# A decoder layer on one core: two projections of the input matrix by seven half-size products, with the operand sums made by ScalarE copies and adding transfers

## What is computed

```python
h = rms_norm(x, ln_mix_g[l])
a_q, a_k, a_v, b_a, b_g, c_q, c_kv, c_kr, d_u = jnp.split(h @ w_in[l], split_at, axis=-1)
q = rms_norm(a_q.reshape(b, s, SWA_HEADS, SWA_HEAD_DIM), swa_qn_g[l])
o_a = swa_sink_attention(q, k, v, swa_sinks[l], rel_bias)
o_b = conformer_conv(b_a, b_g, ...)
o_c = mla_attention(c_q, c_kv, c_kr, ...)        # c_q is RMS-normalised first
o_d = s5_mixer(d_u, ...)
x = x + o @ w_out[l]
x = x + memory_cross_attention(rms_norm(x, ln_cross_g[l]), rms_norm(mem, mem_ln_g[l]), ...)
x = x + hier_moe(rms_norm(x, ln_moe_g[l]), ...)  # top-1 group, top-2 of 32 experts
```

## Time and profile before

| | us |
|---|---|
| three timed runs, median (lowest to highest) | 1413.32 (1412.78 to 1415.44) |
| the profiled execution | 1413.58 |
| its span | 1411.8 |
| PE busy in the span | 1210.6 (86%) |
| DVE busy | 593.1 (42%) |
| ACT busy | 208.4 (15%) |
| GpSimd busy | 13.9 (1%) |
| bytes moved | 477.79 MB, mean 338 GB/s |

### The profile page before, as it was taken

How to read it: one execution, slowest core, us unless ns; L and a number is a source line. 1 busy time by engine, 2 the same in 40 slices (tenths; PEclk the granted TensorE clock), 3 DMA queues, 4 the chain that set the end, 5 groups by cost and what they waited for, 6 DMA issues and landing times.

```text
span 1411.8 us, 16085 instructions
## 1 busy us (share of the span) xinstructions
PE 1210.6 (86%) x6731; PEld 566.3 (40%) x6731; DVE 593.1 (42%) x1222; ACT 208.4 (15%) x461; POOL 13.9 (1%) x31
## 2 busy tenths in 40 slices
PE   8999999999999999887667978777878687787777
PEld 4785565656885632322222222222322222222223
DVE  5999984858754442331122322222222222222222
ACT  3311023351022411100000000000001000000001
POOL 3000000000000000000000000000000000000000
PEclk9999999999999999998888988888889878988898
DMA  9343454333556879999999999999999999999998
GB/s 288 140 150 132 155 190 169 130 120 138 180 239 233 308 312 431 432 431 434 429 431 431 430 431 428 433 431 431 430 431 432 431 431 430 430 431 430 431 424 318
DMA packets 62728, 477.79 MB, mean 338 GB/s; under 512 B 13701, under 2 KB 21253, under 8 KB 45504
## 3 DMA queue, kind: packets, MB, share of 16 engines
q1 hardware_dynamic: 61392, 476.40, 81.8%
q0 software_dynamic: 864, 0.25, 0.3%
q10 hardware_dynamic: 400, 0.10, 0.0%
HBM read 474.63 MB, written 2.11 MB: 338 GB/s over the span
## 4 chain that ended last, share of the span: by engine, by line
PE 58%; DMA 36%; DVE 3%; ACT 2%; issue 1%; SPq 1%; DVEq 0%; ACTq 0%
DMA ring<-in_moe_w_up_dram 20%; DMA late_ring<-in_moe_w_up_dram 14%; PE bank L1294 11%; PE bank L733 10%; PE bank L1329 7%; PE bank L748 5%; PE bank L1050 5%; PE bank L1315 2%; PE bank L717 2%; PE bank L1253 2%; PE bank L1174 2%; PE bank L798 2%; PE bank L1130 2%; PE bank L1019 2%; DMA ring<-in_moe_w_down_dram 1%; PE bank L1366 1%
## 5 line engine op out<-in xcount | busy, mean ns | idle before, releaser
L1294 PE MATMUL bank<-ring,x_gathered 128*32 128x512 f32 x1184 | 252.2, 680 | 52.0 <-DMA late_ring<-in_moe_w_up_dram 36.0
L1294 PE MATMUL bank<-late_ring,x_gathered 128*32 128x512 f32 x800 | 202.3, 682 | 38.8 <-DMA ring<-in_moe_w_up_dram 37.4
L2760 DVE TENSOR_TENSOR tokens_out<-tokens_out,bank 128x512 f32<-128x512 f32 x240 | 148.5, 680 | 202.6 <-PE bank L1366 202.6
L2743 DVE SCALAR_TENSOR_TENSOR hidden<-hidden,bank 128x128 f32<-128x128 f32 x31 | 8.9, 287 | 338.8 <-ACT hidden L1898 338.8
L733 PE MATMUL bank<-ring,hT 128*128 128x512 f32 (+2 forms) x384 | 142.1, 530 | 0.1
L1294 PEld LDWEIGHTS bank<-ring,x_gathered 128*32 128x32 f32 x1184 | 67.0, 123 | 142.2 <-issue 137.5
L1253 PE MATMUL bank<-x_tok,select 128*32 128x512 f32 x512 | 115.9, 1032 | 7.3 <-DVE select L2652 4.2
L1329 PE MATMUL bank<-ring,hidden 128*32 128x512 f32 x560 | 89.1, 793 | 18.2 <-DVE hidden L2745 18.2
L733 PEld LDWEIGHTS bank<-ring,hT 128*128 128x128 f32 x384 | 72.7, 190 | 66.9 <-issue 59.6
L1294 PEld LDWEIGHTS bank<-late_ring,x_gathered 128*32 128x32 f32 x800 | 53.3, 123 | 111.4 <-issue 108.9
L1366 PE MATMUL bank<-y_slots,weight_slots 32*128 32x512 f32 x496 | 72.0, 651 | 28.8 <-ACT y_slots L1913 21.0
(11 more groups left out here) (472 smaller groups left out, 1235.0 us busy)
## 6 DMA issues: line engine op xcount, KB each, us to landing
ring<-in_moe_w_up_dram SPq DMA_DIRECT2D x19, 4096.0 KB, 40.3
ring<-in_moe_w_down_dram SPq DMA_DIRECT2D x16, 4096.0 KB, 29.6
ring<-in_moe_w_gate_dram SPq DMA_DIRECT2D x16, 4096.0 KB, 38.9
late_ring<-in_moe_w_down_dram SPq DMA_DIRECT2D x13, 4096.0 KB, 29.6
late_ring<-in_moe_w_gate_dram SPq DMA_DIRECT2D x12, 4096.0 KB, 39.6
late_ring<-in_moe_w_up_dram SPq DMA_DIRECT2D x10, 4096.0 KB, 38.1
ring<-in_w_in_dram SPq DMA_DIRECT2D x20, 1024.0 KB, 8.1
ring<-in_w_out_dram SPq DMA_DIRECT2D x16, 1024.0 KB, 6.5
```

The lines of the kernel that those rows point to most:

```text
L1294: mm = pe.matmul(gu_bank[SLOTS * c:SLOTS * c + SLOTS, :], XGT[:, at, n % 4, n // 4, :], pieces[c % 2][:, FF * (n % 8):FF * (n % 8) + FF], ...
L2760: ins = v.tensor_tensor(y, x, mix[c][:, :], ALU.add)
```

## The change

The two projections `cq` and `sq` are each cut in four by halves: tokens (0, 1), contraction (two sides of eight slices, 0 and 1) and columns (two halves of 256). With seven products of 128 tokens x 1024 x 256 columns (`seven`, eight matmuls of 256 moving columns each) instead of eight, and sums and differences of the operands and of the results, the same 256 x 512 block comes out.

- **Token sums** T1 to T4 (128 x 8 x 128, 0.5 MB) are made once and used by both groups; **weight sums** S1 to S4 (128 x 8 x 256, 1 MB) once for each group. Each sum is made in two steps: ACT copies one operand, with its sign, to the place of the sum (`part`, L1757 of the new kernel, semaphore `parts_ready`), and GpSimd issues a transfer that adds the other operand to it (`accumulate`, `accum_op=add`); for the token sums from `hT` in SBUF, for the weight sums from `w_in` in HBM once more. 12 copies and 12 adding transfers, 10 MB in all. S2 is made from S1 and S4 from S2 (sign turned by the copy), and GpSimd issues S3 after S1 has landed and S2 after S3 has landed.
- PE takes the products of a group in the order a0, b0 (on plain operands), d1 (T3, S3), c (T1, S1), b1 (T4), a1 (T2, S2), d0 (S4).
- ACT drains four banks for each group; DVE joins them by five operations (`join_seven`).
- **Order.** The groups are now loaded and multiplied in the order ckv, skv, `y1`, cq, sq. `mT0` and `mT1` follow one another directly. SP loads sq pieces 2 and 3, which take the place of cq pieces 0 and 1, after product c of cq.
- The gains of the memory tokens get a tile of their own; the two early constants share one semaphore, so DVE waits for both before its first use of one of them.

Diff, cut:

```diff
-    w = [(g, q) for g in ("u", "za", "zg", "cq", "ckv", "sq", "skv") for q in range(4)]
+    w = [(g, q) for g in ("u", "za", "zg", "ckv", "skv", "cq", "sq") for q in range(4)]
...
+        T8 = [scr[:, a:a + 1024].rearrange("p (k t) -> p k t", k=8) for a in (10240, 8192, 11264, 9216)]
+        S8 = {"cq": [eights(GB[:, :]), eights(scr[:, 0:2048])], "sq": [eights(scr[:, 2048:4096]), eights(GB[:, :])]}
...
-                    if g in ("za", "sq") and q < 2:
+                    if g in ("za", "skv") and q < 2:
                         sp.wait_ge(s["half_used"], 1 if g == "za" else 2)
+                    elif g in ("cq", "sq") and q < 2:
+                        wait_filled(sp, g + "c")
...
-                sp.dma_start(KF[:, :], const_d[:, N_KEPT:N_CONST]).then_inc(s["front_const_in"], 16)
+                sp.dma_start(KF[:, :], const_d[:, N_KEPT:N_CONST]).then_inc(s["const_in"], 16)
...
+            def accumulate(ready, dst, src, name):
+                pool.wait_ge(s["parts_ready"], ready)
+                pool.dma_start(dst, src, accum_op=ALU.add).then_inc(s[SUMMED[name][0]], 16)
...
+            accumulate(1, t1, hT8(1, 1), "T1")
+            accumulate(2, c1, block8_source("cq", 0, 1), "cqS1")
+            accumulate(3, t3, hT8(0, 0), "T3")
+            wait_sum(pool, "cqS1")
+            accumulate(4, block8("cq", 0, 1), block8_source("cq", 1, 1), "cqS3")
+            accumulate(5, t2, hT8(0, 0), "T2")
+            wait_sum(pool, "cqS3")
+            accumulate(6, c2, block8_source("cq", 1, 1), "cqS2")
+            accumulate(7, t4, hT8(1, 0), "T4")
+            wait_sum(pool, "T3")
+            accumulate(8, q1, block8_source("sq", 0, 1), "sqS1")
+            accumulate(9, block8("cq", 1, 0), block8_source("cq", 1, 0), "cqS4")
+            wait_sum(pool, "T4")
+            accumulate(10, block8("sq", 0, 1), block8_source("sq", 1, 1), "sqS3")
+            accumulate(11, q2, block8_source("sq", 1, 1), "sqS2")
+            accumulate(12, block8("sq", 1, 0), block8_source("sq", 1, 0), "sqS4")
...
-            projection("cq", 512)
+            def seven(g):
+                def by8(b, x, w):
+                    for j in range(8):
+                        mm = pe.matmul(b, x[:, j, :], w[:, j, :], start=j == 0, stop=j == 7)
+                    return mm
...
+                by8(a[:, 0:T], hT8(0, 0), block8(g, 0, 0))
+                by8(b[:, 0:T], hT8(1, 0), block8(g, 1, 0)).then_inc(s["half_used"], 1)
+                wait_sum(pe, "T3")
+                wait_sum(pe, g + "S3")
+                by8(d[:, T:2 * T], t3, block8(g, 0, 1))
+                wait_sum(pe, "T1")
+                wait_sum(pe, g + "S1")
+                filled(by8(c[:, 0:T], t1, s1))
+                wait_sum(pe, "T4")
+                filled(by8(b[:, T:2 * T], t4, block8(g, 1, 1)))
+                wait_sum(pe, "T2")
+                wait_sum(pe, g + "S2")
+                filled(by8(a[:, T:2 * T], t2, s2))
+                wait_sum(pe, g + "S4")
+                filled(by8(d[:, 0:T], hT8(1, 1), block8(g, 1, 0)))
             projection("ckv", 320)
-            projection("sq", 512)
             projection("skv", 256)
+            c_products(1)
+            seven("cq")
+            seven("sq")
             pe.wait_ge(s["mem_in"], 16)
             model_transposes("mT", 0, xn_of[0])
-            c_products(1)
...
+            act.wait_ge(s["scan_done"], 5)
+            part(t1, hT8(0, 1), 1.0)
+            pieces_arrived("cq", 0)
+            part(c1, block8("cq", 0, 0), -1.0)
+            part(t3, hT8(0, 1), -1.0)
+            part(block8("cq", 0, 1), block8("cq", 0, 1), -1.0)
             act.wait_ge(s["dist_out"], 16)
             for tt in range(TT):
                 drain(f"skv{tt}", SKV[:, tt, :], cols=256, scale=ROWS[:, tt:tt + 1])
+            act.wait_ge(s["scan_done"], 8)
+            wait_sum(act, "T1")
+            part(t2, t1, -1.0)
+            drain("y1", OT[:, 14:16, :], four(2))
+            wait_sum(act, "cqS1")
+            part(c2, c1, -1.0)
+            wait_sum(act, "T2")
+            part(t4, t2, 1.0)
+            pieces_arrived("sq", 0)
+            part(q1, block8("sq", 0, 0), -1.0)
+            wait_sum(act, "cqS2")
+            act.wait_ge(s["half_used"], 3)
+            part(block8("cq", 1, 0), c2, -1.0)
+            part(block8("sq", 0, 1), block8("sq", 0, 1), -1.0)
+            wait_filled(act, "cqc")
+            wait_sum(act, "sqS1")
+            part(q2, q1, -1.0)
+            drain_seven("cq")
+            wait_sum(act, "sqS2")
+            act.wait_ge(s["half_used"], 4)
+            part(block8("sq", 1, 0), q2, -1.0)
+            drain_seven("sq")
...
-            wait_task(dve, "ckv1")
+            join_seven("cq")
...
-            wait_task(dve, "skv1")
+            join_seven("sq")
```

83 lines of the change are left out of this document (65 added, 18 removed).

## The result

| | before | after |
|---|---|---|
| timed runs, median (lowest to highest), us | 1413.38 (1412.78 to 1415.44) | 1450.48 (1447.48 to 1454.21) |
| ratio, 95% interval | | 1.0259 (1.0247 to 1.0272) |
| profiled execution, us | 1413.58 | 1447.92 |
| its span, us | 1411.8 | 1446.0 |

The change costs 37 us. It was forecast to cost 16, with 1447 as the upper end of the range: the direction was right, the size was not.

A forecast was written before the change was run, and what follows sets the result against it. PE was taken to bound the front, one to one to the end: -6.9 + 0.5 + 1.2 + 19.9 = +14.7, with about 1.5 for slower pieces and clock +16, from 1413.6 to 1430 us; range 1409 to 1447.

The forecast's parts named there:

- Removed and added on PE, -6.9: Projections cq and sq on PE: seven half-width products save 3.4 us a group, 6.9 us in all, if no product waits.
- Order and transposes, +0.5 and +1.2: PE waits about 0.5 us for skv's late pieces, and 1.2 us ahead of xv0 for the drains of mT0.
- One to one to the end: A microsecond on PE in the front moves the end by one, since early expert loads wait for a PE task.
- DVE's joins at nothing: Five join operations a group on DVE, 2.6 us, lie under other work and cost nothing; uncovered, 5 us.
- S1's start, 140: cq's first weight sum is issued at 140 us, after cq piece 1 arrives, T1's transfer and a copy of about 2.0 us.
- Landings: 1 MB adding transfers land in 8.3 us, plus 2.6 sharing for S1 and S4; waits in d1, b1, d0 total 19.9 us.
- "The group sq has its sums made in that time and I give it no wait.": sq's operand sums are made during cq's waits, so sq's products on PE wait 0 us.
- Clock after waits, 1.5 with the slower pieces: Lower TensorE clock after waits, together with the slower 1 KB pieces, adds about 1.5 us.
- Constants, nothing: The joint wait for two constants delays DVE's early work by half a microsecond under PE's work, at no cost.
- Signs of being wrong: Landings of 5 us, S transfers not slowed by SP's loads, or a later front without a later end.
- the two rules weighed ahead: Adding transfers run at about half a copy's rate (5.2 us of data), against GpSimd's 2.0 us plus bytes at 436 GB/s (4.4 us).
- three turns: Rival: two reads and the write in turn, 10.9 us an adding transfer, d0 35 us late, 1446 us; chance 0.17 (or worse).

The follow-up runs named there:

- narrow_first: Kernel before the change with only the new order (ckv, skv, y1, cq, sq as plain projections, memory transposes in a row): 1416.44 us.
- no_transfers: Changed kernel without its 12 adding transfers, TensorE waiting only for ScalarE's copies; stretch from zg1's end to xv0 87.84 us, whole time (1443.67 us) not comparable.
- gpsimd_adds: Changed kernel with the 12 sums made by GpSimd additions on blocks already in SBUF, without copies or transfers: 1455.3 us.
- loads_later: Changed kernel with SyncE issuing the first piece of sq only after cqS3 has landed: 1453.99 us.
- price_probe: Changed kernel with four more GpSimd transfers, run one by one in idle stretches (512 KB and 1 MB, each plain and adding): 1447.84 us.
- const_merged: Kernel before the change with only the edit to the constants (one shared semaphore, waits for both loads): 1414.37 us.
- s1_early: Changed kernel with cqS1 made early, from a block loaded at about 54 us, its adding transfer in the idle stretch behind 87 us: 1442.14 us.
- one_block_early: Changed kernel with only cq by seven products, behind sq's plain projection; cqS1 made before the projections, cqS2 issued before cq's pieces arrive: 1422.14 us.
- plain_copies_b: Changed kernel with GpSimd's 12 transfers as plain copies, same places and waits, run once more for a profile: 1432.8 us.

## Why the prediction was wrong, and where it was right

- **Removed and added on PE, -6.9.** Right: 6.87 us between narrow_first and no_transfers.
- **Order and transposes, +0.5 and +1.2.** Right: 0.63 and 1.30 us of waits; narrow_first's stretch has 0.7 us more, which stays unplaced.
- **One to one to the end.** Right: 1211.1 to 1212.1 us behind xv0 in every kernel that routes alike, gpsimd_adds apart.
- **DVE's joins at nothing.** Right: the five operations of cq's join took 2.7 us (205.06 to 207.74), and PE waits for no norm.
- **S1's start, 140.** It was 142.46: piece 1 landed at 140.16, not 137 to 138, and ScalarE's copy came behind that. T1's transfer is the smaller part of it: in no_transfers, which has none, the copy starts at 139.39 instead of 140.25. The four pieces themselves took about 12 us from their release, not 10.
- **Landings: the step that failed.** The data term of an adding transfer, at half a copy's rate, was right (8.3 assumed, 8.9 alone; in the changed kernel cqS3 took 9.3 and cqS2 10.2). What failed is the sharing, taken as 2.6 us for S1 and S4 and as nothing elsewhere. Measured: 16.1 for cqS1, 17.5 for sqS1, 17.7 for cqS4. loads_later took 5 us off cqS1 by moving the loads, and the loads fell on another. In the prediction's own chain: cqS2 was issued at 168.28 instead of 159 (2.5 us by S1's start, 5.2 by cqS1, 1.0 by cqS3, the rest in the steps between), and from there to d0 it took 30.1 us instead of the 24 that were counted for the queue, so d0 ran at 198.4 instead of 183. I reasoned about each transfer and never summed the stage: twelve adding transfers, 10.5 MB at 200 GB/s, are 52 us of DMA time (some 57 with the token sums at the 143 GB/s of price_probe), and some 8 MB of loads 20 more, in a stretch of 58 us between S1's issue and the old start of xv0. The engines were all but full from 142 to 206 us, with one gap of about 2 us at 160. That sum could have been made from the prediction's own 5.2 us a megabyte. It is 14 to 19 us too long for the stretch, less than the 30 us that PE waited; that the rest comes of the order in which the sums depend on one another and stand in GpSimd's queue is argued, and the order of the queue was not tested by itself.
- **"The group sq has its sums made in that time and I give it no wait."** Nearly right by luck: sq waited 0.95 us, because PE itself was 30 us late.
- **Clock after waits, 1.5 with the slower pieces.** The products behind the waits took 6.0 us more than at full clock.
- **Constants, nothing.** Not refuted: const_merged is 0.7 us above the kernel before, with an interval that takes in no change.
- **Signs of being wrong.** None of the three came: no landing of 5 us, S transfers slowed by loads, front and end later together. They would have told a wrong mechanism, and it was a size that was wrong.

The sum with measured sizes: -6.9 for the products, 30.1 of waits for sums (16.8 + 4.7 + 7.7 + 0.95), 6.0 of clock, 1.9 of waits by the order, and 1.8 unplaced (0.7 of it in narrow_first too) make the 32.9 of the stretch; 1.0 ahead of it and 0.3 behind make the 34.2 of the span. The timed median lies 2.6 us above the profiled execution, within what the runs of this kernel spread (1447.5 to 1454.2).

On the two rules weighed ahead: the trace sides with the half rate of Collectives: The Full Stack in the Trainium skill, section The bandwidth ceiling (200 GB/s while only adding transfers move, 399 for loads; out of SBUF 143 against 287). The 4.4 us for 1 MB, estimated from DMA: Bandwidth & Descriptors in the Trainium skill, section Anatomy of one DMA, are not reached even by a lone plain copy of GpSimd (5.9).

Of the rivals, "three turns" gave nearly the right time (1446) by a wrong price: a lone transfer doesn't take 10.9 us, a shared one takes more.

## What to carry to other kernels

Before work is moved to transfers, sum the DMA time of the whole stretch (each adding megabyte counts as two of copying) and hold it against the stretch's length; a dependent transfer beside loads must be priced at the rate that is left, here 16 to 18 us where it took 9 alone. A chain of such transfers can be hidden only where its operands exist early; taking the chain's first links ahead (s1_early, one_block_early) gave back 8 to 9 us of the kernel each time, and moving only the loads gave nothing. An operation with an eighth less arithmetic isn't cheaper if its operands have to be made by the resource that the rest of the stage also waits for.

## What the runs showed of the hardware

- **An adding transfer is cut into small packets.** 12,480 packets for 10.49 MB (840 bytes each) against 2,752 for the same bytes as plain copies (3.8 KB). GpSimd needs 1.55 us to issue one (the rows of one_block_early) and 0.9 for a plain one (in plain_copies_b).
- **It takes about twice as long when it shares.** cqS1, cqS2 or cqS3, whichever runs beside loads, takes 16 to 19 us, 7 to 10 more than alone, while the loads of 1 MB in this stretch land in 10.6 us (median; 11.1 beside the plain copies). Loads are slowed as well: the two that follow product c took 6.1 us without transfers, 14.4 beside adding ones and 14.8 beside plain ones. The Trainium skill, DMA: Bandwidth & Descriptors, section Queues, rings and completion order, says that an engine turns between its queues packet by packet; small packets against larger ones would then get the smaller part of the bytes. The lengthened adding transfers agree with that in direction; the loads, slowed as much by plain copies as by adding ones, don't show it, and it wasn't tested by itself.
- **GpSimd's arithmetic shuts DVE out for whole operations**, 4.1 us for one that took 0.41 us before (L2313 in gpsimd_adds, 4085 ns each). This operation has one input tensor and a column of scalars, so the sentence on two SBUF inputs cited above doesn't cover it.
- **TensorE's granted clock fell to 0.50 within a wait of 17 us**, and the product of eight behind it took 5.6 instead of 3.6 us.
